# One core, two transformer blocks: the first modulation in two halves with table tiles between, the end of the second modulation at the second norm, and shared banks in the banded half

## The reference, cut to what matters

```
def ada_params(cvec, w, b):
    m = jax.nn.silu(cvec) @ w + b
    return jnp.split(m, 3, axis=-1)          # shift, scale, gate

def modulate(x, g, shift, scale):
    return rms_norm(x, g) * (1.0 + scale) + shift

# first block, layer i
shift, scale, gate = ada_params(c, ada_w[i], ada_b[i])
h = modulate(x_lat, norm_g[i], shift, scale)
...                                          # proj = h @ w_in, mixer, y
x_lat = x_lat + gate * y

# second block, even layer, second half of the heads
valid = (jnp.abs(qpos - kpos) <= WINDOW) & (kpos >= 0) & (kpos < s_len)
s = jnp.where(valid, s, NEG_INF)             # blocks of 128, up to 3 of keys
```

## Time and profile before

| | us |
|---|---|
| median of 3 runs | 2472.72 (2471.39 to 2475.32) |
| the profiled execution | 2473.51, its span 2471.7 |
| TensorE busy | 2430.0 (98%) |
| GpSimd, VectorE, ScalarE busy | 1634.4, 1094.9, 661.7 |
| matmuls of the table helper (L620) | 1641.3 and 1033.6 |

### The profile page before, as it was taken

How to read it: one execution, slowest core, us unless ns; L and a number is a source line. 1 busy time by engine, 2 the same in 40 slices (tenths; PEclk the granted TensorE clock), 3 DMA queues, 4 the chain that set the end, 5 groups by cost and what they waited for, 6 DMA issues and landing times.

```text
span 2471.7 us, 32481 instructions
## 1 busy us (share of the span) xinstructions
PE 2430.0 (98%) x11582; PEld 1970.8 (80%) x11582; DVE 1094.9 (44%) x1487; ACT 661.7 (27%) x1264; POOL 1634.4 (66%) x1432
## 2 busy tenths in 40 slices
PE   7999999999999999999999999999999999999998
PEld 4886678888888887778888888888888788888886
DVE  5455644454333227865433323433326567433312
ACT  4264521112111006652111101111112564211100
POOL 3555946666667777546666777666777766666775
PEclk9999999999999999999999999999999999999999
DMA  7313632333333333103333333333333222333332
GB/s 270 116 60 136 206 110 94 94 101 94 93 102 93 102 103 93 30 10 103 100 95 94 101 107 98 97 98 93 103 109 107 88 80 68 95 93 101 94 102 85
DMA packets 68947, 248.43 MB, mean 101 GB/s; under 512 B 7424, under 2 KB 9984, under 8 KB 68224
## 3 DMA queue, kind: packets, MB, share of 16 engines
q1 hardware_dynamic: 63808, 232.81, 30.1%
q10 hardware_dynamic: 5056, 14.51, 1.6%
HBM read 245.19 MB, written 2.10 MB: 100 GB/s over the span
## 4 chain that ended last, share of the span: by engine, by line
PE 95%; DVE 2%; ACT 1%; DMA 1%; POOL 1%; issue 1%; DVEq 0%; ACTq 0%; SPq 0%; POOLq 0%
PE pb L620 74%; PE pb L1224 4%; PE pb L1165 2%; PE pb L921 2%; PE pb L1089 2%; PE pb L804 1%; PE pb L629 1%; PE pb L1071 1%; PE pb L1055 1%; PE pb L1207 1%; PE pb L848 1%; PE pb L1194 1%; PE pb L1240 1%; PE pb L1181 1%; PE pb L872 1%; PE pb L835 1%
## 5 line engine op out<-in xcount | busy, mean ns | idle before, releaser
L620 PE MATMUL pb<-ar,w_hi 128*128 128x512 f32 x5312 | 1641.3, 390 | 0.9 <-POOL w_lo L451 0.6
L620 PEld LDWEIGHTS pb<-ar,w_hi 128*128 128x128 f32 x5312 | 994.3, 188 | 217.0 <-issue 6.2
L620 PE MATMUL pb<-ar,w_lo 128*128 128x512 f32 x2656 | 1033.6, 389 | 0.0
L451 POOL TENSOR_TENSOR w_lo<-raw,w_hi 128x1024 fp32r<-128x1024 f32 x379 | 949.5, 2505 | 31.6
L620 PEld LDWEIGHTS pb<-ar,w_lo 128*128 128x128 f32 x2656 | 498.6, 188 | 104.2
L448 POOL TENSOR_TENSOR still<-still 128x1 f32<-128x1 f32 x392 | 82.3, 210 | 685.1 <-PE pb L620 541.4
L449 POOL TENSOR_SCALAR w_hi<-raw 128x1024 fp32r<-128x1024 f32 x379 | 403.9, 1066 | 0.0
L2148 DVE TENSOR_TENSOR tb<-pb,nb 128x512 f32<-128x512 f32 x88 | 60.9, 692 | 380.8 <-PE pb L620 380.8
L2154 DVE TENSOR_TENSOR ar<-tb,ar 128x512 f32 x88 | 156.1, 1774 | 90.9 <-ACT ar L1556 90.9
L2037 DVE SCALAR_TENSOR_TENSOR x<-pb,x 128x512 f32<-128x512 f32 x48 | 36.2, 757 | 345.8 <-PE pb L620 341.3
L1556 ACT ACTIVATE ar<-tb 128x512 f32 x88 | 55.7, 633 | 494.4 <-DVE tb L2151 494.4
(11 more groups left out here) (275 smaller groups left out, 2370.4 us busy)
## 6 DMA issues: line engine op xcount, KB each, us to landing
raw<-wstream SPq DMA_DIRECT2D x427, 512.0 KB, 3.6
raw<-wstream SPq DMA_DIRECT2D x4, 1024.0 KB, 10.7
x<-xt ACTq DMA_DIRECT2D x2, 2048.0 KB, 10.0
tb<-wstream SPq DMA_DIRECT2D x2, 1024.0 KB, 11.7
rt<-wstream SPq DMA_DIRECT2D x2, 1024.0 KB, 11.7
out<-x ACTq DMA_DIRECT2D x8, 256.0 KB, 2.2
rt<-nbias ACTq DMA_DIRECT2D x4, 384.0 KB, 3.8
nb<-nbias ACTq DMA_DIRECT2D x4, 384.0 KB, 3.6
```

The lines of the kernel that those rows point to most:

```text
L451: pool.tensor_tensor(lo, src, hi.bitcast(F32), ALU.subtract).then_inc(s_split, 1)
L620: mm = pe.matmul(pb[:, bank, :], weights(a, n, t)[:, k * P:(k + 1) * P], rhs(b, k0 + k), start=(first and k == 0 and i == 0), stop=(last a ...
```

## The change

Three parts, with nothing else touched.

1. **First modulation in two halves.** The pairs are fetched and multiplied in the order 0, 1, 4, 5, 2, 3, 6, 7: shift and scale of features 0 to 511 first, in bank 0, then those of the others in bank 3. Only four pairs fit at first; the fifth goes to the place of the third once that is multiplied, and so on. The first halves of three `gate_in` groups are fetched ahead of pair 4, their second halves behind pair 7. Copy, fold, `modulation` and row tiles run for each half. TensorE's order is: four pairs, gains, norm sum, filler, fold, pair 4 (counted from 0), filler, column 0 of three `gate_in` tiles, pair 5, column 1, pairs 6 and 7, column 2 with the second fold inside, columns 3 to 5, then columns 6 and 7 of each tile. VectorE multiplies x by the root four tiles at a time.
2. **Second modulation.** ADA_PAIRS has 13 pairs, at u = 3 to 15. The last six groups go in three fetches to `rt`, `tb[0:4]` and `tb[4:8]`, issued by SyncE behind the last fetch of `even_out`, and are multiplied at the second norm: one pair between the two sum matmuls, two behind them; a second copy and fold stand at column 2 of the `odd_in` tiles, and VectorE adds the result to `par[72:80]`. The rope table is fetched whole behind that norm.
3. **Shared banks.** In the banded half both sides of blocks 0 and 3 go to one bank, and each turn waits for the turn that last held its place, 3 to 5 turns back; ScalarE and VectorE wait for both sides in those blocks.

```diff
-        ADA_PAIRS = (0, 0, 2, 1, 1, 1, 1, 1, 1, 1, 1, 1, 1, 1, 1, 1, 1)
+        ADA_PAIRS = (0, 0, 0, 1, 1, 1, 1, 1, 1, 1, 1, 1, 1, 1, 1, 1)
...
+        def turned(n):
+            w, side = divmod(n, 2)
+            if w < 16:
+                return T_BANKS[n % 3], 0, n - 3
+            a, b, c = T_BANKS[2], T_BANKS[0], T_BANKS[1]
+            if w % 4 == 0:
+                return a, 2 * P * side, max(2 * w - 4, 29)
+            if w % 4 == 1:
+                return (c, 0, 2 * w - 3) if side else (b, 0, max(2 * w - 5, 30))
+            if w % 4 == 2:
+                return (b, 0, 2 * w - 2) if side else (a, 0, 2 * w - 3)
+            return c, 2 * P * side, 2 * w - 3
...
+        ADA0_ORDER = (0, 1, 4, 5, 2, 3, 6, 7)
+        ADA0_PLACE = (0, 1, 2, 3, 2, 3, 2, 3)
+        EARLY = 3
...
+            for i, p in enumerate(ADA0_ORDER):
+                if i == 4:
+                    for j in range(EARLY):
+                        sp.wait_ge(s_ada, 2 * (j // 2) + 2)
+                        sp.dma_start(raw[:, j, 0:TOK], wstream[RAW0["gate_in"] + j][:, 0:TOK]).then_inc(s_early[j], 16)
+                if i >= 4:
+                    sp.wait_ge(s_ada, 2 * (i - 2) + 2)
+                sp.dma_start(ADA0[ADA0_PLACE[i]].rearrange("p (g c) -> p g c", g=2),
+                             wstream[2 * p:2 * p + 2].rearrange("g p c -> p g c")).then_inc(s_ada0[ADA0_PLACE[i]], 16)
...
+                if seg == "even_out":
+                    sp.wait_ge(at["o"], 8)
+                    sp.wait_ge(at["oad"], 4)
+                    sp.wait_ge(s_split, SPL0["even_out"] + 1)
+                    for p in range(3):
+                        g = RAW0["ada1"] + GATE2 + 2 * p
+                        sp.dma_start(GATE2_HOME[p].rearrange("p (g c) -> p g c", g=2),
+                                     wstream[g:g + 2].rearrange("g p c -> p g c")).then_inc(s_gate2[p], 16)
...
+            gate_column(0)
+            ada0_pair(5)
+            gate_column(1)
+            ada0_pair(6)
+            ada0_pair(7)
+            gate_column(2, fold_second_half)
+            gate_column(3)
+            gate_column(4)
+            gate_column(5)
+            for i in range(EARLY):
+                for k in range(6, KT):
+                    h_ready("n0")(k)
+                    for q in range(3):
+                        mm = gate_step(i, k, q)
+                mm.then_inc(s_group, 1)
...
-            sum_squares_late("n1", 3)
-            side_by_side(3, TILE0["odd_in"], SPL0["odd_in"], lambda b, k: H[b][:, k, :], "n1")
+            sum_squares_late("n1", 2, between=lambda: second_gate(0))
+            for p in range(1, 3):
+                second_gate(p)
+            def turn_second_gate():
+                pe.wait_ge(s_row, 4)
+                fold_rows(tb[:, 7, :], 7)
+            side_by_side(3, TILE0["odd_in"], SPL0["odd_in"], lambda b, k: H[b][:, k, :], "n1", extra=turn_second_gate)
...
-                    if n >= 3:
-                        pe.wait_ge(bt["lo"], n - 2)
+                    if n >= 3:
+                        pe.wait_ge(bt["lo"], turned(n)[2] + 1)
...
-            act.wait_ge(s_ada, COUNT["ada0"])
-            act.activation(tb[:, 2, :], pb[:, 0, :], ACT.Copy).then_inc(s_row, 1)
+            for half in range(2):
+                act.wait_ge(s_ada, 8 + 8 * half)
+                if half:
+                    act.wait_ge(s_turned, 1)
+                act.activation(tb[:, 2, :], pb[:, 3 * half, :], ACT.Copy).then_inc(s_row, 1)
...
+            for half in range(2):
+                for k in range(4 * half, 4 * half + 4):
+                    dve.tensor_tensor(x[:, k, :], x[:, k, :], rstd, ALU.mult).then_inc(s_xr, 1)
+                dve.wait_ge(s_turned, half + 1)
+                modulation(0, half)
+                dve.wait_ge(s_xr, 4 + 4 * half)
+                n0_even(4 * half)
+                n0_lo(4 * half)
+                n0_even(4 * half + 2)
+                for k in range(4 * half + 1, 4 * half + 4):
+                    n0_lo(k)
```

More of the change, by code:

```diff
@@ L429, in _ @@
                             load(t * RAW + (RAW0[seg] + j), j)
+                if seg == "ada1":
+                    for j in range(GATE2 % RAW):
+                        free(seg, groups + j - RAW)
+                        load(RAW0[seg] + groups + j, j)
+                if seg == "even_out":
[6 more added lines that the diff above has]
+                                     wstream[g:g + 2].rearrange("g p c -> p g c")).then_inc(s_gate2[p], 16)
         @block.gpsimd
@@ L590, in _ @@
                     for half in range(2):
-                        for j in range(SPLIT):
+                        for j in range(EARLY):
                             split_half(g0 + j, n0 + j, half, j + 1)
-                for j in range(SPLIT if seg == "gate_in" else 0, RAW):
+                for j in range(EARLY if seg == "gate_in" else 0, RAW):
                     split(g0 + j, n0 + j, guard=seg != "gate_in", pairs=seg in ("k", "q"),
@@ new lines, in ada0_pair @@
+            def ada0_pair(i):
+                p, bank = ADA0_ORDER[i], 0 if i < 4 else 3
+                place = ADA0_PLACE[i]
+                pe.wait_ge(s_ada0[place], 16 * ADA0_USE[i])
+                for c in range(4):
+                    g, kk = 2 * p + c // 2, c % 2
+                    k, q = 2 * (g % 4) + kk, g // 4
+                    mm = pe.matmul(pb[32 * c:32 * c + 32, bank, :], C_WIN[:, k, 6 - 2 * q:38 - 2 * q],
+                                   ADA0[place][:, c * TOK:(c + 1) * TOK], start=(i % 4 == 0), stop=(i % 4 == 3))
@@ L699, in _ @@
                     if kk == 1:
                         mm.then_inc(s_ada, 1)
-                if p in (5, 6):
-                    between(TOK)
-                if p == 7:
-                    between(TOK // 2)
+            pe.wait_ge(s_csil, 1)
+            for i in range(4):
+                ada0_pair(i)
+            gains = vec[:, VEC["q_g"]:VEC["q_g"] + 4]
+            pe.wait_ge(s_ld["mat"], 16)
+            pe.matmul(pb[:, 5, 0:4], by_pairs, gains, start=True, stop=True)
+            pe.matmul(pb[:, 5, 4:8], by_partners, gains, start=True, stop=True).then_inc(s_gains, 1)
@@ L706, in ada_pair @@
+            sum_squares("n0")
+            between(TOK)
             def ada_pair(u):
@@ L1538, in _ @@
             hi_tiles("n1", 56)
+            act.dma_start(rt[:, :, :], rope).then_inc(s_ld["rope2"], 16)
             with act.Fori(0, 8) as t:
```

200 lines of the change are left out of this document (114 added, 86 removed).

## The result

The change made the kernel slower, where I had forecast 2469.5 us and put 0.08 on slower by over 0.2%.

The account below looks back on a forecast made before the run. TensorE, busy 98% of 2471.7 us, was taken as the bound. Front and second modulation gave -0.7 and the banded half -2.5, so -3.2: 2470.3 us profiled, 2469.5 median, range 2467 to 2472.

Parts of the forecast that it names:

- The sum: Whole kernel: -0.7 and -2.5 make -3.2 us, 2470.3 for the profiled execution, 2469.5 for a median; chance 0.45.
- the new holes: TensorE idle: 2.2 us in the front, 2.5 at u = 2, 2.2 at the fifth output tile.
- the third rival: Clock falls in the new holes: one fall 2472.1 us, two 2474.7, three 2477.3; chance 0.12 for two or more.
- the last pair's arrival: Front: the last weight pair lands at 37.9 us, TensorE waits 2.2 for it, and the pair ends at 38.9.
- the wait for `x`: Fifth output tile: `x` takes 11.4 us and lands at 316.0, so TensorE waits 2.2.
- The front: First modulation in halves: first table matmul 4.7 us earlier, mostly lost to the last pair; 0.2 gained, bounds -2.4 to +0.7.
- The steps up to the fold: Front: norm's sum ends at 23.9 us, VectorE's first product at 25.4, fold done at 27.2.
- The second modulation: Attention to second norm: pairs moved out, `x` late, clock kept up at the norm, a second fold added; -0.5 us.
- The attention: Three pairs leave it: -1.0 us for the pair of u = 16, -0.1 for the two of u = 2.
- The norm: Second norm: moved pairs fill the hole and the clock stays up, -2.6 us; the new second fold costs +1.06.
- The banded half: Last block of each head: four waits for a bank copy shrink by 0.63 us each, -2.5, between 0 and -3.2.

Follow-up runs that it names:

- the part alone: The kernel before with only the first modulation in two halves: 2475.77 us, ratio 1.0013 [1.0004, 1.0022], 3.7 slower.
- part 2 alone: The kernel before with only the last six groups of the second modulation moved to the second norm: 2475.85 us, ratio 1.0012 [1.0003, 1.0021], 3.8 slower.

## Why the prediction was wrong

Between the forecast for the profiled execution (3.2 faster) and what it measured (6.6 slower) lie 9.8 us: 6.0 in the front, 3.8 at the fifth output tile, 1.4 at the norm, less 1.4 elsewhere. The step that failed is the clock. The sum put falls in the new holes at nothing, and the third rival gave two or more of them 0.12, because each hole was shorter than the 2.9 of the earlier trace rows. In this profile falls make some 4.3 in the front, 1.6 behind `x` and 1.6 at the norm (25.7 instead of 24.1), 7.5 of the 9.8. The two other terms that were too small are the last pair's arrival (2.0) and the wait for `x` (1.9).

**The front** (forecast -0.2, the part alone +3.7). The steps up to the fold held, and came up to 0.8 early: sum at 22.24, fold at 25.33. VectorE's four products took 3.98, not 2.45, beside GpSimd's splits (the other four, with GpSimd idle, 2.49), and the first table matmul came at 30.24, not 29.5. I had read the 2.62 of the earlier trace rows and allowed 0.2 for it; the same operation without a split beside it shows what the meeting costs:

```profile
69.14 0.48 DVE L1785 SCALAR_TENSOR_TENSOR ar<-tb,par,ar 128x256 fp32r<-128x256 f32 x1
```

SyncE issued the last fetch at 33.67, not 32.6; it took 6.2, not 5.3 (in other executions 4.9 to 5.8), and the wait was 3.07, not 2.2. The last pair started at 39.91, 2.0 behind the forecast. Then the clock: at this place it fell behind 3.07, 2.67, 2.58, 2.27 and 1.86, and cost by estimate some 1.6 us where it stayed low for 3.4 and some 4.3 where it stayed for 10 (the 9.1 us from 39.91 to 49.0, at 0.43 a matmul instead of 0.227). That a wait behind table work was the root is shown: moving one pair ahead of it gave back 3.0 us. What share of those the clock has is not settled, since filling the wait alone changed the spread but hardly the median.

**The second modulation** (forecast -0.5, alone +3.8). The late `x` was in the sum, by the right mechanism, and I had its price too low. `x` took 12.2, not 11.4. And I had taken its issue and TensorE to move together, but against TensorE's work it was issued 1.2 later: before, 313.16 - 305.90 = 7.3 us ahead of the landmark, after 317.63 - 311.54 = 6.1. The rows of VectorE's last step but one in the attention, and of GpSimd's split beside it, show where the 1.2 comes from. Before, then after:

```profile
303.05 1.21 DVE L2002 SCALAR_TENSOR_TENSOR nb<-nb 128x512 f32<-128x512 f32 x1 [2.06 <-ACT nb L1461]
```
```profile
301.32 2.40 POOL L451 TENSOR_TENSOR ar<-raw,ar 128x1024 fp32r<-128x1024 f32 x1
```
```profile
307.52 2.38 DVE L2121 SCALAR_TENSOR_TENSOR nb<-nb 128x512 f32<-128x512 f32 x1 [3.40 <-ACT nb L1579]
```
```profile
306.96 2.40 POOL L502 TENSOR_TENSOR ar<-raw,ar 128x1024 fp32r<-128x1024 f32 x1
```

The step starts as soon after TensorE's last sum matmul as before, and ends 0.5 to 0.6 us behind the end of the split, in all 19 profiles; `x` is issued 2.2 behind that end, in all 19. So by these rows the split sets the issue. With part 2 TensorE is earlier against the splits, and the step meets 1.8 us of one instead of 0.7: it takes 2.38 to 2.40 in all 14 profiles with part 2, 1.21 to 1.26 in the five without. No run moved the split, so this is read from the traces and not tested.

So 3.5 + 1.2 less 0.5 of slack make the 4.1 (I had 2.2), and the clock's fall 1.6 behind it; it fell in all eight profiles with a wait of 3.5 to 4.4 here, and in none with 1.3 or less. Putting the fetches behind `x` undid most of the longer fetch and the fall: 3.4 us. The wait of 1.3 that stays is the 1.2 of the later issue and 0.7 of longer fetch, less the slack. The attention gave 1.3 here (I had 1.1), but that agreement is luck: in 12 of 14 profiles the clock fell in the new hole at u = 2, as the third rival had it, and the average gain is 0.7. The norm gave 0.2 in the profile, where its clock fell, and 1.8 where it stayed up (I had 1.6), against one long fall before.

The Trainium skill (DMA: Bandwidth & Descriptors, "Issuing engines are not separate DMA queues") says that transfers of different engines interleave on the same 16. The trace agrees: 12.2 and 12.0 us with the fetches ahead, 9.4 with them behind.

**The banded half** (forecast -2.5): right, -2.7, and by the mechanism named.

## What to carry to other kernels

Ahead of an order change, ask of each wait that bounds the end what issues it: `x` hung on a VectorE step that ended with a GpSimd split, and gained nothing from a shorter TensorE; and a fetch into a place hangs on the work that is queued ahead of its last reader. Put the reader ahead of the optional work, and bulk that is needed later behind the transfer that is needed next, in the same queue. Price a new hole in a stretch of full speed with the clock's fall behind it, also where it is shorter than the one hole seen; and read a stretch in several profiles before you take its gain from one.

## What was not expected of the hardware

- The same fall lasts 3.4 us in one execution and 10.2 in another of the same kernel (0.83 and 0.50 mean clock from 39 to 49). At the context sum its two profiles are 3.0 us apart.
- No length of hole separates falls from none: the clock fell behind 1.86, 2.58 and 3.07 at the last pair and stayed up behind 1.61 there (the kernel with five fillers in the wait for pair 1); at u = 2 it fell behind 2.41 in 12 profiles of 13, and stayed up behind 2.70 in that of part 2 alone; at the norm, behind 1.07 and 0.52, it fell in four profiles and stayed up in nine with the same holes.
- Half speed at the start is not in the granted clock: it reads 1.00 while a pair takes 1.93. Without fillers in the first waits, it ended at 18 to 34 us.
- Two VectorE steps that ran beside a GpSimd split lasted until it had ended: one took 2.62 us instead of 0.48 and ended 0.3 behind the split, the other 2.38 instead of 1.21 and ended 0.5 behind it. The split took its 2.4 both times.
